# A reordered opening, other PSUM banks for a norm, and a final norm over turned sums in pieces of 512, 384 and 136 tokens

## What is computed

```python
x = x + 0.5 * swiglu(rmsnorm(x, ffn1_norm), ffn1_w_gate, ffn1_w_up, ffn1_w_down)
# a mixing layer: input projection, an RG-LRU scan, a chunked SSD scan, output projection
x = x + concat([lru_out, ssd_out]) @ w_out
x = x + 0.5 * swiglu(rmsnorm(x, ffn2_norm), ffn2_w_gate, ffn2_w_up, ffn2_w_down)
y = rmsnorm(x, final_norm)      # x * rsqrt(mean(x * x) + 1e-6) * gain
```

## Time and profile before

| | us |
|---|---|
| median of 3 runs | 2143.51 (2143.16 to 2144.99) |
| the profiled execution, its own time | 2143.93 |
| its span, first to last instruction | 2142.2 |

### The profile page before, as it was taken

How to read it: one execution, slowest core, us unless ns; L and a number is a source line. 1 busy time by engine, 2 the same in 40 slices (tenths; PEclk the granted TensorE clock), 3 DMA queues, 4 the chain that set the end, 5 groups by cost and what they waited for, 6 DMA issues and landing times.

```text
span 2142.2 us, 36204 instructions
## 1 busy us (share of the span) xinstructions
PE 2123.9 (99%) x15368; PEld 2092.2 (98%) x15368; DVE 1376.1 (64%) x1268; ACT 739.9 (35%) x1096; POOL 900.1 (42%) x534
## 2 busy tenths in 40 slices
PE   9999999999999999999999999999999999999998
PEld 9999999999999999999999999999999999999998
DVE  7887776771223557878888596786767667641216
ACT  6423223230001224678786540133322322410004
POOL 4555445443433323343534553233644444433440
PEclk9999999999999999999999999999999999999999
DMA  5122122263322322311112332132222222353212
GB/s 170 61 99 79 60 100 80 80 206 121 99 72 83 132 80 81 138 44 40 53 42 81 138 99 73 50 119 80 80 79 81 79 75 85 139 188 99 93 56 80
DMA packets 64753, 197.81 MB, mean 92 GB/s; under 512 B 9416, under 2 KB 18120, under 8 KB 64592
## 3 DMA queue, kind: packets, MB, share of 16 engines
q1 hardware_dynamic: 63440, 194.97, 26.6%
q10 hardware_dynamic: 1152, 0.52, 0.1%
HBM read 149.37 MB, written 46.26 MB: 91 GB/s over the span
## 4 chain that ended last, share of the span: by engine, by line
PE 90%; DVE 3%; ACT 2%; DVEq 1%; issue 1%; DMA 1%; POOL 0%; ACTq 0%; SPq 0%; POOLq 0%
PE banks L786 44%; PE banks L891 38%; PE banks L830 3%; PE banks L1140 2%; DMA w_raw<-in_gate_up 0%; PE banks L1058 0%; ACT gate_a L1396 0%; PE banks L1054 0%; PE banks L1036 0%; ACT gate_x L1396 0%; DVEq L1979 0%; PE banks L1028 0%; DVE decay L2014 0%; DMA x<-in_xt 0%; PE banks L1061 0%
## 5 line engine op out<-in xcount | busy, mean ns | idle before, releaser
L655 POOL TENSOR_SCALAR w_hi<-w_raw 128x1024 fp32r<-128x1024 f32 (+1 forms) x93 | 106.5, 1146 | 570.7 <-PE banks L786 507.4
L657 POOL TENSOR_TENSOR w_lo<-w_raw,w_hi 128x1024 fp32r<-128x1024 f32 (+1 forms) x100 | 273.3, 2733 | 161.8 <-DVE xbc L1985 123.7
L786 PE MATMUL banks<-h_hi,w_lo 128*128 128x344 f32 x948 | 303.8, 321 | 2.3 <-DVE up L1673 2.3
L786 PE MATMUL banks<-h_lo,w_hi 128*128 128x344 f32 x948 | 303.1, 320 | 0.0
L786 PE MATMUL banks<-h_hi,w_hi 128*128 128x344 f32 x948 | 302.8, 319 | 0.0
L786 PE MATMUL banks<-u_hi,w_lo 128*128 128x344 f32 x864 | 285.7, 331 | 0.7 <-DVE lru_even L1594 0.4
L786 PE MATMUL banks<-u_hi,w_hi 128*128 128x344 f32 x864 | 275.9, 319 | 0.0
L786 PE MATMUL banks<-u_lo,w_hi 128*128 128x344 f32 x864 | 275.6, 319 | 0.0
L1749 DVE SCALAR_TENSOR_TENSOR x<-banks,x 128x1032 f32<-128x1032 f32 x42 | 51.8, 1232 | 321.0 <-PE banks L786 321.0
L786 PEld LDWEIGHTS banks<-h_hi,w_lo 128*128 128x128 f32 x948 | 178.1, 188 | 2.7 <-DVE up L1673 2.7
L786 PEld LDWEIGHTS banks<-h_hi,w_hi 128*128 128x128 f32 x948 | 178.5, 188 | 0.0
(11 more groups left out here) (353 smaller groups left out, 5615.6 us busy)
## 6 DMA issues: line engine op xcount, KB each, us to landing
w_raw<-in_gate_up SPq DMA_DIRECT2D x46, 512.0 KB, 4.4
hidden<-up SPq DMA_DIRECT2D x44, 516.0 KB, 3.6
stage<-hidden SPq DMA_DIRECT2D x44, 516.0 KB, 3.8
raw<-in_gate_up SPq DMA_DIRECT2D x40, 512.0 KB, 4.3
w_raw<-in_w_in SPq DMA_DIRECT2D x36, 512.0 KB, 4.3
w_raw<-in_down SPq DMA_DIRECT2D x32, 512.0 KB, 4.6
x<-in_xt SPq DMA_DIRECT2D x16, 516.0 KB, 6.5
x_kept<-x SPq DMA_DIRECT2D x16, 516.0 KB, 5.2
```

Of the source, the lines that this page charges most:

```text
L655: pool.tensor_scalar(w_hi[s][:, 0:n], w_raw[s][:, 0:n], 1.0, 0.0, ALU.mult, ALU.add)
L657: pool.tensor_tensor(w_lo[s][:, 0:n], w_raw[s][:, 0:n], w_hi[s][:, 0:n].bitcast(F32), ALU.subtract).then_inc(split, 1)
L786: end = pe.matmul(out[:, c, 0:CH], w[s][:, k * P:(k + 1) * P], x[kx][:, c * CH:(c + 1) * CH], start=(first and n == 0), stop=(last and n = ...
```

## The change

It reorders the opening's products and adds one warming matmul; gives the high parts of the second gate and up units to ACT; puts `norm_turned` ahead of all four `mix_low`; moves the norm of FFN 2 to banks 6, 7 and 2; spreads the `hidden_low` of the last group one to a join, with 5 to 7 behind the join of p4, and lets the second down product start without its wait; and does the final norm with tokens on the partitions, in pieces of 512, 384 and 136.

```diff
-PIECES = [slice(0, 376), slice(376, 752), slice(752, T)]
+PIECES = [slice(0, 512), slice(512, 896), slice(896, T)]
...
-        f1.n_at, f2.n_at = banks[:, 2:5, :], sets[s]
+        f1.n_at, f1.n_end = banks[:, 2:4, :], banks[:, 4, :]
+        f2.n_at, f2.n_end = pair, banks[:, 2, :]
...
+        def piece_chunks(c):
+            return [(t // QC, t, min(QC, T - t)) for t in range(PIECES[c].start, PIECES[c].stop, QC)]
...
+                elif name in (("g1", 1), ("u1", 1)):
+                    pool.wait_ge(first_high_parts, u + 3)
...
-                    elif o == (1 if f.tag == "1" else 0):
+                    elif o == 1:
                         pe.wait_ge(*f.rooted.past(3))
...
-                        if b == 0 and m < 2:
-                            pe.wait_ge(*f.ev.past(6 * NG - 1 + m))
+                        if b == 0 and m == 0:
+                            pe.wait_ge(*f.ev.past(read_number(NG - 1, "p3")))
...
-            for _ in range(12):
+            for _ in range(13):
...
-            for k in range(KT):
-                highs(g, gate, k)
-                highs(u, up, k)
-            for k in range(KT):
+            high(g, gate, 0)
+            high(u, up, 0)
+            weight_low(g, gate, 0)
+            low(g, gate, 0)
+            low(u, up, 0)
+            weight_low(u, up, 0)
+            for k in range(1, SIDE // P):
+                for unit, out in ((g, gate), (u, up)):
+                    high(unit, out, k)
+                    weight_low(unit, out, k)
                 low(g, gate, k)
-            for k in range(KT):
                 low(u, up, k)
+            for unit, out in ((g, gate), (u, up)):
+                for k in range(SIDE // P, KT):
+                    high(unit, out, k)
+                    weight_low(unit, out, k)
+                    low(unit, out, k)
...
             def last_sum(c):
                 here, end = PIECES[c], c == CHUNKS - 1
-                out = pair[:, c % 2, 0:here.stop - here.start]
                 pe.wait_ge(added["final"], (KT - 1) * (c + 1) - end)
                 if end:
-
-                    pe.wait_ge(root_taken, 1)
-                    pe.matmul(out, ones[:], f2.tot[:, here], start=True, stop=False)
                     pe.wait_ge(squared["final"], CHUNKS * KT)
-                pe.matmul(out, ones[:], (f2.c[(KT - 1) % 2] if end else f2.tot)[:, here], start=not end,
-                          stop=True).then_inc(summed["final"], 1)
+                parts = (f2.tot, f2.c[(KT - 1) % 2]) if end else (f2.tot,)
+                if c >= 2:
+                    pe.wait_ge(y_done_final, KT // 2 * (c - 1))
+                for j, (_, t, rows) in enumerate(piece_chunks(c)):
+                    for n, part in enumerate(parts):
+                        last = pe.matmul(pair[0:rows, c % 2, 8 * j:8 * j + 8], part[:, t:t + rows], ones[:, 0:8],
+                                         start=(n == 0), stop=(n == len(parts) - 1))
+                last.then_inc(summed["final"], 1)
+
+            def last_spread(c):
+                pe.wait_ge(root_taken, 2 * (c + 1))
+                for j, t, rows in piece_chunks(c):
+                    at = t - PIECES[c].start
+                    last = pe.matmul(pair[:, c % 2, at:at + rows], turned[0:rows, j:j + 1].broadcast_to([rows, P]),
+                                     ident[0:rows, 0:rows], start=True, stop=True)
+                last.then_inc(summed["final"], 1)
...
                     if c and m == WHOLE:
                         last_sum(c - 1)
+                    if c and m == WHOLE + 1:
+                        last_spread(c - 1)
             last_sum(CHUNKS - 1)
+            last_spread(CHUNKS - 1)
...
+            def second_weights(name):
+                u = U(name)
+                act.wait_ge(used, u - 1)
+                act.wait_ge(landed[u % 2], 32)
+                act.activation(w_hi[u % 2][:], w_raw[u % 2][:], ACT.Copy).then_inc(first_high_parts, 1)
+
+            second_weights(("g1", 1))
             taken(f1, ("g1", 0), f1.g_at, f1.g[0][0])
...
             act.wait_ge(*f1.mix_ready.past(2))
+            second_weights(("u1", 1))
             taken(f1, ("u1", 0), f1.u_at, f1.u[0])
...
             for c in range(CHUNKS):
                 for m in range(KT):
-                    piece_square(c, m)
                     if c and m == WHOLE:
                         piece_root(c - 1)
+                    piece_square(c, m)
...
-                    for j in range(6, 8):
+                    for j in range(5, 8):
                         hidden_low(f, j)
...
-            for k in range(2):
-                mix_low(f1, k)
             norm_turned(f1)
-            for k in range(2, 4):
+            for k in range(4):
                 mix_low(f1, k)
...
             def piece_scale(c, k):
...
                 if k == 0:
-                    dve.wait_ge(root_taken, c + 1)
-                    dve.reciprocal(rstd[:, here], rstd[:, here])
-                    dve.drain()
+                    dve.wait_ge(summed["final"], 2 * c + 2)
...
+            def piece_root(c):
+                first, full, _ = piece_sums(c)
+                dve.wait_ge(root_taken, 2 * c + 1)
+                end = dve.reciprocal(turned[:, first:full], turned[:, first:full])
...
                     piece_residual(c, m)
-                    if c and 3 <= m < 7:
-                        piece_scale(c - 1, 2 * (m - 3))
+                    if c and m == WHOLE:
+                        piece_root(c - 1)
+                    if c and m >= 4:
+                        piece_scale(c - 1, 2 * (m - 4))
                     if (c, m) != (CHUNKS - 1, KT - 1):
                         piece_add(c, m)
```

More of the change, by code:

```diff
@@ L410, in piece_bank, with piece_sums @@
             return sets[s][:, (m - WHOLE) % 3, 0:here.stop - here.start]
+        def piece_chunks(c):
+            return [(t // QC, t, min(QC, T - t)) for t in range(PIECES[c].start, PIECES[c].stop, QC)]
+        def piece_sums(c):
+            first, full = PIECES[c].start // QC, PIECES[c].stop // QC
+            return first, full, pair[:, c % 2, 0:8 * (full - first)].rearrange("p (j n) -> p j n", n=8)[:, :, 0]
+        rest = 8 * (NCH - PIECES[CHUNKS - 1].start // QC)
+        last_rows = pair[0:DEC, (CHUNKS - 1) % 2, rest:rest + 1]
         def sync(sp):
@@ L846, in norm_spread @@
                     rows = QC if c < NCH else DEC
-                    end = pe.matmul(f.n_at[:, c // 4, c % 4 * QC:c % 4 * QC + rows],
+                    to = f.n_at[:, c // 4, c % 4 * QC:c % 4 * QC + rows] if c < NCH else f.n_end[:, 0:rows]
+                    end = pe.matmul(to,
                                     turned[0:rows, c:c + 1].broadcast_to([rows, P]), ident[0:rows, 0:rows],
@@ L912, in tensor, with high @@
             gate, up = f1.g_at, f1.u_at
-            def highs(unit, out, k):
+            def high(unit, out, k):
                 if k == 0:
-                    pe.wait_ge(half_split, unit + 1)
+                    pe.wait_ge(first_high_parts, unit + 1)
                 if k == SIDE // P:
@@ L919, in highs, with weight_low @@
                 pe.wait_ge(x_hi_done, k + 1)
[L920 to L923, removed]
+                for c in range(CHUNKS):
+                    pe.matmul(out[:, c, :], w_hi[unit][:, k * P:(k + 1) * P], flat(f1.bh[k])[:, c * CH:(c + 1) * CH],
+                              start=(k == 0), stop=False)
+            def weight_low(unit, out, k):
+                if k == 0:
+                    pe.wait_ge(half_split, unit + 1)
+                for c in range(CHUNKS):
+                    pe.matmul(out[:, c, :], w_lo[unit][:, k * P:(k + 1) * P], flat(f1.bh[k])[:, c * CH:(c + 1) * CH],
+                              start=False, stop=False)
             def low(unit, out, k):
@@ L1193, in norm_spread @@
                 act.wait_ge(summed[name], 2)
-                act.activation(halves(rstd[:, 0:PROMPT]), f.n_at[:, 0:2, :], ACT.Copy)
-                act.activation(rstd[:, PROMPT:T], f.n_at[:, 2, 0:DEC], ACT.Copy).then_inc(f.rooted.sem, 1)
+                act.activation(halves(rstd[:, 0:PROMPT]), f.n_at, ACT.Copy)
+                act.activation(rstd[:, PROMPT:T], f.n_end[:, 0:DEC], ACT.Copy).then_inc(f.rooted.sem, 1)
             def operand_high(f, o):
@@ L1564, in piece_root @@
             def piece_root(c):
[L1565 to L1568, removed]
+                act.wait_ge(summed["final"], 2 * c + 1)
+                first, full, sums = piece_sums(c)
+                end = act.activation(turned[:, first:full], sums, ACT.Sqrt, bias=eps[:, 0:1], scale=1.0 / DM)
+                if c == CHUNKS - 1:
+                    end = act.activation(turned[0:DEC, NCH:TOK], last_rows, ACT.Sqrt, bias=eps[0:DEC, 0:1], scale=1.0 / DM)
+                end.then_inc(root_taken, 1)
             for c in range(CHUNKS):
                 for m in range(KT):
-                    piece_square(c, m)
                     if c and m == WHOLE:
                         piece_root(c - 1)
```

(19 more changed lines are left out.)

1 line of the change is left out of this document (added).

## The result

| | before | after |
|---|---|---|
| median of 6 runs, us | 2144.09 (2142.93 to 2145.23) | 2153.01 (2151.0 to 2153.67) |
| the profiled execution, its own time and span | 2143.93, 2142.2 | 2152.9, 2151.2 |
| first piece starts in the chain | 2079.41 | 2074.21 |
| last multiply ends, counted from there | 59.57 | 74.05 |

The ratio is 1.004 (95% interval 1.003 to 1.005): 8.9 us slower, where 3.4 us faster was forecast. The third and fourth line of the table already say where to look. TensorE comes to the final pieces 5.2 us earlier than before, and from there to the last multiply it takes 14.5 us longer.

A forecast was written before the change was run, and what follows sets the result against it. TensorE, busy 99% of the span, was taken to bound the kernel. Gains of 3.3 (opening), 1.2 (norm banks) and 2.35 (joins) less 3.5 us (end) make 3.35 us less: forecast 2140.3 us, range 2137.4 to 2143.3.

The forecast's parts named there:

- Opening: Reordered products of the opening: TensorE runs without gap or half clock, gaining 3.3 us (bounds 2.2 and 3.8).
- Rival C: Opening: half clock comes all the same, or VectorE's total or `mix_low` are later; 2141.3 to 2142.5 us, chance 0.18.
- Norm banks: FFN 2: the first group product no longer waits for the copies of the norm, gaining 1.2 us (bounds 1.1 and 1.2).
- Joins: Last group of both FFNs: the first down product's wait for a VectorE join goes, gaining 2.35 us (bounds 2.3 and 2.4).
- that join starts 2.0 to 2.4 us earlier: Last group: with one `hidden_low` moved behind, the join of p3 starts that much earlier, under the last product.
- The end on TensorE: Final pieces: TensorE's products, sums and spreads end 59.7 us after the first piece's start, before 52.3.
- rival A: Third piece: short matmuls hide their weight loads, 0.064 us each in proportion; 2137.4 to 2138.3 us, chance 0.18.
- rival B: Third piece: short float32r matmuls fall to the float32 rate, 0.227 us each; about 2152.5 us, chance 0.09.
- I take 0.11 us: 11.9 us for 108: Third piece: each 136-token matmul is bound by its weight load, where proportion gives 6.9 us for 108.
- the second sum waits about 0.5 us: End of the second piece: `piece_scale` stands ahead of the last `piece_add`, so TensorE's second final sum waits.
- Behind the last product: After TensorE's last product: residual, sum, roots, reciprocals, spread and multiplies take 4.2 us, about 4.3 with the semaphores.
- The smaller stores: Last stores after the last multiply: 139 KB instead of 280 KB, taking 2.4 us for 3.2, a gain of 0.8.

The follow-up runs named there:

- e3: The changed kernel with the last `piece_add` of the second piece ahead of `piece_scale`, so no wait ahead of the second sum: 2143.20 us.
- e8: The changed kernel's front only, with the final norm and the pieces of 376, 376 and 280 of before: 2137.72 us.
- e12: The changed kernel with the final sums' matmuls moving 128 columns of ones instead of 8: 2143.59 us.
- e6: The changed kernel with two float32 matmuls, result not read, ahead of the wait for the second final sum: 2143.60 us.
- e1: The changed kernel with pieces of 384, 384 and 264 tokens: 2140.53 us.
- e2: The changed kernel with the third piece's products moving 264 columns instead of 136, the extra ones not read: 2144.29 us.
- e5: The kernel of e2 with one more 0.30 us VectorE operation ahead of the second piece's last add, restoring the wait: 2144.66 us.
- e11: The kernel of e3 with a wait put in ahead of tile 5 of the third piece, away from the sums: 2144.00 us.

## Why the prediction was wrong

**Opening: right.** Forecast 3.3 us within 2.2 to 3.8; measured 3.93 at the first group product less the wait of 0.24 behind it, 3.7. Two terms were off. VectorE's total, forecast to be 0.8 us late, ended 1.5 us ahead of its use; the last `mix_low` ended at 63.49, forecast 62.7, which makes the wait of 0.24. In e3, e8 and e12 that wait is 0.7 to 0.9 us, and the opening gives 3.2 to 3.3. Rival C is refuted in its main form, as the windows at 9.00 and 13.50 show full clock.

**Norm banks: right.** Forecast 1.2 us; in the chain after, the spread ends at 1471.41 and the first group product starts at once.

**Joins: too high.** Forecast 2.35 us, measured 1.8: 0.9 in either FFN. I moved the joins forward by half of a pair of stretched `hidden_low` (4.89 us), which gave 2.44, but a single one alone takes 2.89 or 3.25 us. The step that failed is "that join starts 2.0 to 2.4 us earlier": in FFN 2 it starts 403.4 us behind the first group product, before 404.3, so 0.9 us earlier.

**The end on TensorE: right in all but the clock.** With the clock held the last product ends 59.8 us after the first piece's start (e6: 2134.47 less 2074.67; e12 has the same), forecast 59.7. The wait of 0.5 us was forecast and came. A 136-token matmul every 0.111 us is the forecast 0.11, so neither rival A (0.064) nor rival B (0.227 at full clock) is what happened. The Trainium skill (TensorE: Matmul & The Clock Gate, Back-to-back issue gap) has 81 ns for such a stream at 128 columns; this trace disagrees for float32r operands at 136 columns, with 111 ns, and the sum rightly did not go by it.

**The step that failed** is the pair of sentences "I take 0.11 us: 11.9 us for 108" and "the second sum waits about 0.5 us". Both numbers are right, and I priced them apart, at full clock. The opening had just been read as an idle stretch that is followed by half clock, and I did not ask it of the new wait. The wait, together with the sparse sum and the thin products, brings the clock to half for the rest of TensorE's work. Term by term against e6: the last 72 products 15.26 for 8.00, tile 3 of the piece 2.86 for 2.06, the spreads 1.38 for 0.72 and 1.33 for 0.81, the last sum 1.20 for 0.78. That is 9.7 us in the profiles, and 9.4 between the medians.

**Behind the last product: a little low.** Forecast 4.3 us to the last multiply, in e6 4.6 (2134.47 to 2139.08): the sum took 0.78 for 0.6 and the spread 0.81 for 0.45, roots and reciprocals 0.69 for 0.8. (The terms written in the prediction add up to 4.05, not 4.2.) The smaller stores gave 0.3 us, not 0.8: the span ends 2.9 us behind the last multiply, before 3.2. The end's cost at full clock is thus 64.4 - 59.6 - 0.3 = 4.5 us, forecast 3.5, and it is 14.2 as it ran.

**The sum again, against the span.** Gains of 3.7 + 1.17 + 1.8 = 6.7, less 1.5 for the short fall at 786, less 14.2, is 9.0 slower: 2151.2 against 2142.2. The terms are read from the same two profiles, so this only says that none is missing. Had only the clock held at the end, the change would have lain about 1 us under before (e6 and e12 have 2143.6), and 0.3 above the upper end of my range: the joins, the tail behind the last product, the stores and the fall in the mixing layer take the rest.

**The rivals.** The time is close to rival B's 2152.5, but that is an accident. B says that short matmuls are slow by themselves, and e3 has 108 of them at 0.111 us. A half clock stood in my list for the opening only (rival C), where it did not come.

**What stays open.** Besides e1, six edits of the end prevented the fall (e2, e3, e5, e6, e11, e12), and several of these also add columns or take away idleness near 2122. So "each of the three is needed" stands for these edits; that they act as three separate causes is argued. What exactly the chip adds up, and how far the change is from the edge, was not measured: no run halved the wait or the sums, and none made only the products ahead of the wait, or only those behind it, wide. Nor was it shown that the place of the wait in time is without influence; the six runs of the change speak for that. Nor is it settled that the 8-column sums differ from denser ones by their columns and not by the timing of their weight loads.

## What to carry to other kernels

A wait, a thin stream and a handful of tiny matmuls can each be harmless and together cost many times the wait, as they did here (0.5 us of waiting, 9.4 us lost). So price a wait that an edit adds to TensorE together with what surrounds it, and read the granted clock ahead of the busy share: 99% busy stood in both profiles. If such a place can't be avoided, take one of the three away: the cheapest here was to put the short dependent add ahead of the long multiply on VectorE (e3), or to fill the wait with matmuls that nobody reads (e6). Faster still was a choice of pieces that makes neither thin products nor the wait (e1, 2140.53).

And test the parts of a bundle alone. Three of the four parts here were worth 6 to 7 us, and the fourth hid them.

## What the runs showed of the hardware that I had not expected

- The clock fell behind an idle stretch of 0.5 us only, with six sparse passes and thin products beside it. Before, the fall in the opening stood behind 1.26 us.
- The load of 128 weight columns follows the clock: 0.19 us long at full clock and 0.33 at half, and a stream that it bounds comes every 0.111 and 0.213 us. In proportion to the 0.172 us of 376 tokens, the 136 columns of the matmul itself would need 0.062 us at full clock and, by an estimate of twice that, 0.124 at half. So at either clock it seems to be the load that sets the pace. The Trainium skill (TensorE: Matmul & The Clock Gate, LDWEIGHTS) has one figure for both, the columns over 1.2, which agrees at full clock (0.107) and is half of what the rows at half clock show.
- The clock may or may not fall for a stretch behind a run of 64 matmuls of 8 columns, in profiles of equal code up to there. In this kernel that is 1.5 to 1.7 us of scatter in the middle, more than many of the terms of this prediction.
